# Expert weights of both layers as 1 MiB transfers throughout, where most went in pairs of 2 MiB

## The reference, cut to what matters

```python
def expert_choice_ffn(h, w_router, w_gate, w_up, w_down):
    b, n, d = h.shape
    cap = max(1, (EC_CAPACITY * n) // N_EXPERTS)          # 32 tokens for each expert
    aff = jax.nn.softmax((h @ w_router).astype(jnp.float32), axis=-1)
    g, idx = lax.top_k(jnp.swapaxes(aff, 1, 2), cap)
    xe = jax.vmap(lambda hb, ib: hb[ib])(h, idx)
    a = jnp.einsum('becd,edf->becf', xe, w_gate)
    up = jnp.einsum('becd,edf->becf', xe, w_up)
    y = jnp.einsum('becf,efd->becd', jax.nn.silu(a) * up, w_down) * g[..., None].astype(h.dtype)
    return jax.vmap(lambda ib, yb: jnp.zeros((n, d), h.dtype).at[ib.reshape(-1)].add(yb.reshape(-1, d)))(idx, y)
```

## Time and profile before

| | |
|---|---|
| median of 3 runs | 2635.04 us (2633.99 to 2636.32) |
| the profiled execution | 2635.41 us, its span 2634.1 us |
| PE busy | 2511.8 us (95%) |
| PEld (weight loads of PE) busy | 1543.5 us (59%) |
| DVE / ACT / POOL busy | 1182.1 / 437.4 / 92.7 us |
| moved by DMA | 690.06 MB, mean 262 GB/s |
| issued at line 745 in one piece of 2048 KB | 122 into `ring`, 9 + 9 + 8 into `ring_low`, `ring_high`, `ring_far` |
| granted clock of PE | 0.997 of full speed |

### The profile page before, as it was taken

One profiled execution on the slowest core, in us unless ns is written; L12 is line 12 of the kernel. 1 busy time (PEld: TensorE's weight loads), 2 busy tenths in 40 slices (PEclk: granted clock), 3 DMA queues, 4 the chain that ended last, 5 costly groups with the idle time before them and its releaser, 6 DMA issues.

```text
span 2634.1 us, 27251 instructions
## 1 busy us (share of the span) xinstructions
PE 2511.8 (95%) x11522; PEld 1543.5 (59%) x11522; DVE 1182.1 (45%) x1973; ACT 437.4 (17%) x878; POOL 92.7 (4%) x69
## 2 busy tenths in 40 slices
PE   9999999889999999987879999999999999999999
PEld 5344343424368843332338857888866875878884
DVE  4971321212165521110117755546656665553664
ACT  2111100001132210000001101531101111260110
POOL 0011000000000000000000110001001001001000
PEclk9999999999999999999999999999999999999999
DMA  9853999999962599999997653324444744333441
GB/s 370 323 221 156 393 427 425 428 427 428 425 279 79 205 365 428 427 426 428 426 424 230 194 191 144 112 86 191 171 176 156 196 176 160 128 112 128 170 181 65
DMA packets 93335, 690.06 MB, mean 262 GB/s; under 512 B 25621, under 2 KB 28053, under 8 KB 29469
## 3 DMA queue, kind: packets, MB, share of 16 engines
q1 hardware_dynamic: 90720, 682.66, 65.1%
q0 software_dynamic: 848, 2.90, 0.4%
q10 hardware_dynamic: 1644, 2.76, 0.3%
HBM read 687.22 MB, written 1.06 MB: 261 GB/s over the span
## 4 chain that ended last, share of the span: by engine, by line
PE 82%; DMA 12%; DVE 5%; issue 0%; ACT 0%; POOL 0%; DVEq 0%; POOLq 0%; ACTq 0%
PE bank L772 80%; DMA ring<-in_stream 9%; DMA ring_high<-in_stream 3%; PE bank L775 3%; DVE ab_z L2333 1%; DVE ring L2754 1%; DVE moe_turned L2522 0%; DVE moe_silu L2520 0%; DVE moe_results L2526 0%; DMA vectors<-in_vectors 0%; POOL ab_ln_sum L3058 0%; DVE moe_top L2437 0%; DVE gates L2715 0%; DVE moe_max L2435 0%; DVE normed L2706 0%
## 5 line engine op out<-in xcount | busy, mean ns | idle before, releaser
L772 PE MATMUL bank<-normed,ring 128*128 128x256 f32 (+1 forms) x1824 | 495.3, 428 | 5.0 <-ACT normed L1781 1.6
L772 PEld LDWEIGHTS bank<-normed,ring 128*128 128x128 f32 x1824 | 342.2, 190 | 152.0 <-issue 106.4
L772 PE MATMUL bank<-ring,gates 128*128 128x256 f32 (+1 forms) x1504 | 374.8, 393 | 2.1 <-DVE ring L2754 1.1
L772 PE MATMUL bank<-ring,moe_chosen 128*64 128x512 f32 x1504 | 334.3, 595 | 30.5 <-DMA ring<-in_stream 29.0
L772 PEld LDWEIGHTS bank<-ring,gates 128*128 128x128 f32 x1504 | 282.1, 190 | 60.8 <-issue 23.0
L772 PE MATMUL bank<-ring,normed 128*128 128x256 f32 (+1 forms) x1376 | 313.8, 375 | 0.5 <-DVE cd_rinv L2573 0.5
L772 PEld LDWEIGHTS bank<-ring,normed 128*128 128x128 f32 x1376 | 255.7, 190 | 36.7 <-issue 2.3
L772 PEld LDWEIGHTS bank<-ring,moe_chosen 128*64 128x64 f32 x1504 | 105.5, 137 | 247.9 <-issue 191.6
L2520 DVE TENSOR_TENSOR moe_silu<-bank,moe_silu 128x512 f32<-128x512 f32 x32 | 22.1, 691 | 408.1 <-PE bank L772 408.1
L772 PE MATMUL bank<-ring,moe_turned 128*64 128x512 f32 (+1 forms) x832 | 165.1, 547 | 19.8 <-DVE moe_turned L2522 18.0
L772 PE MATMUL bank<-ring,ffn_hidden 128*128 128x512 f32 x352 | 170.6, 592 | 0.0
(11 more groups left out here) (405 smaller groups left out, 2420.1 us busy)
## 6 DMA issues: line engine op xcount, KB each, us to landing
ring<-in_stream SPq DMA_DIRECT2D x296, 1024.0 KB, 6.9
ring<-in_stream SPq DMA_DIRECT2D x122, 2048.0 KB, 25.6
ring_low<-in_stream SPq DMA_DIRECT2D x9, 2048.0 KB, 39.9
ring_high<-in_stream SPq DMA_DIRECT2D x9, 2048.0 KB, 40.1
ring_far<-in_stream SPq DMA_DIRECT2D x8, 2048.0 KB, 38.2
hidden<-in_stream SPq DMA_DIRECT2D x10, 1024.0 KB, 36.0
normed<-in_stream SPq DMA_DIRECT2D x10, 1024.0 KB, 37.7
ring_filter_freq<-in_stream SPq DMA_DIRECT2D x6, 1024.0 KB, 16.6
```

The lines of the kernel that those rows point to most:

```text
L772: return nc.tensor.matmul(o, lhsT, rhs, start=start, stop=stop, skip_group_check=True)
```

## The change

`SINGLY` names all sixteen experts instead of two, for both layers, so that every entry of `transfers(plan)` is one chunk: each has its own wait, issue, landing semaphore and place in memory as 128 rows of 8 KB. `pack_stream`, which lays the stream out on the host, follows the same list. The order of the stream, the places, and all arithmetic stay as they are.

```diff
--- before.py
+++ after.py
@@ -353,7 +353,7 @@
 AB_COLUMN = {"gate_out": 0, "gate_in": 1, "val": 2, "glu_a": 3, "glu_g": 4}
 
 
-SINGLY = (1, 2)
+SINGLY = tuple(range(NE))
 
 
 def transfers(plan):
```

## The result

The changed kernel takes 2641.41 us (median of 9 runs, 2640.06 to 2642.74), the kernel before 2634.78 us in its 9 runs: ratio 1.0026, 95% interval 1.0018 to 1.0035. The forecast was 2641.9 us, slower than before. The profiled execution took 2641.10 us with a span of 2639.8, that is 5.7 us more than before in both.

A forecast was written before the change was run, and what follows sets the result against it. The prediction took the DMA engines, saturated in both expert stages, to bound the kernel. It added +10.6 us for the lower rate and -3.7 us for shorter tails to 2635.04 us, giving 2641.9 us, range 2635.0 to 2648.0.

The forecast's parts named there:

- The sum: Whole kernel: +10.6 us for the rate and -3.7 us for the tails, +6.9 us in all.
- What binds: Both expert stages: DMA engines never rest (busy share 1.01), so a stage ends when its bytes are through.
- Rival 3: Expert stages: PE's waits for landings set the end; removing 37.9 us of idle time gives 2597 us; chance 0.04.
- The rate: Saturated expert stages: each of 140 pairs costs 0.076 us more as two transfers, +10.6 us.
- The start: Start of both saturated stretches: unmoved, costed at nothing; at most 2.5 us at stake for each stage.
- Whose price it is: Saturated expert stages: shorter rows and a second completion together cost 0.076 us for each pair.
- The tails: Last up pair of each expert stage: half of PE's 3.68 us saved, -1.84 us each, -3.7 us in all.
- The issues: SP's queue: 148 added issues, 49 us, lie within its 2278.6 us of waiting for PE and cost nothing.
- Rival 1: Expert stages: half the price for each pair, +1.6 us in sum, 2636.6 us; chance 0.08.
- Rival 2: Expert stages: no price for the rate, only the tails count, 2.1 us saved, 2632.9 us; chance 0.08.
- Rival 4: Expert stages: single chunks run at 401 GB/s in bulk, +40 us, 2675 us; chance 0.07.
- Rival 5: Expert stages: a fixed 2.2 us for each transfer does not overlap, +308 us, 2943 us; chance 0.01.

The follow-up runs named there:

- experiment 3: The changed kernel, with PE waiting for both landings of a pair before its first matmuls on gate and up weights: 2645.3 us.
- experiment 1: The kernel before, its pairs kept as one transfer, wait and landing each, but moved as rows of 8 KB instead of 16 KB: 2645.4 us.
- experiment 2: The kernel before, each pair issued as two 1 MiB transfers after one wait, PE told only when both have landed: 2645.28 us.
- experiment 9: The kernel before with the change made for the first expert stage alone: 2637.72 us, ratio 1.0011 to the kernel before.
- experiment 4: The changed kernel with each expert chunk moved as 256 rows of 4 KB, still one 1 MiB transfer: 2667.44 us.

## Why the prediction was right, point by point

**The sum.** Forecast +6.9 us, measured +6.6 in the medians. That these agree within 0.3 us is partly luck: the profile has 5.7 us, made of 9.1 for the later landings and -3.4 for the tails, where the forecast had 10.6 and -3.7.

**What binds.** Right. The busy share stayed at 1.01, and every kernel with 8 KB rows ended its stages later by the bytes it moved at the lower rate. (One reading of the chain was off: of its ten DMA pieces nine lie in the expert stages, and one of 5.9 us at the very start of the program. Nothing hangs on it.) Rival 3, that PE's waits for landings set the end, fell: in the five groups of the earlier trace rows PE now idles 26.0 + 2.9 + 3.3 + 2.2 + 1.0 = 35.4 us for DMA instead of 37.9, and with the groups left out there 39.0 instead of 40.6, where the rival wanted nearly all of it gone; and experiment 3, which put the waits for pairs of gate and up weights back, cost the two tails and at most 0.5 us more.

**The rate.** Right in cause, a little large in size. The forecast's 0.076 us for a pair came from a 50 us window. Over 100 us, experiments 1 and 2 measure 0.072 and the changed kernel itself 0.073 (42.04 MB), 10.1 to 10.3 us for 140 pairs. The landings moved by a little less: in the changed kernel by 4.76 + 4.36 = 9.1 us, against 10.6 forecast, or 0.065 us a pair. Experiments 1, 2 and 3 have no gain at the tails and start the FFN 9.4, 10.1 and 9.7 us later than before (1392.51, 1393.23 and 1392.79 instead of 1383.13).

**The start.** Costed at nothing, and within 1 us it was. The first saturated stretch begins as before: no bytes in 267 to 269 us in both, 422 against 421 GB/s behind it. Ahead of the second the queue is idle in both, and bytes flow again some 2 us later than before, where the first stage ended 3.0 us later. Whether the separate waits gain something there is open. In the second stage alone, the two kernels with them lose 4.4 us (the changed kernel and experiment 3) and the two without 5.1 (experiments 1 and 2). But experiment 9, which has the pairs of before in that stage, also comes out 0.5 us better there than before, and one profile of each cannot settle it.

**Whose price it is.** The forecast named shorter rows and the second completion together. Experiments 1, 2 and 4 part them: rows of 16, 8 and 4 KB are moved at 427, 421 and 409 GB/s, whatever the number of transfers, and the completion costs nothing that the medians show. The single packets of the traces say the same. From 500 to 600 us a row of 16 KB takes 615.8 ns on its engine (before), one of 8 KB 314.1 (changed kernel), one of 4 KB 163.8 (experiment 4): two short rows take 12.4 and 13.5 ns longer than one of twice the length. A completion packet takes 9.6 ns. That the rates give only 9 ns a row goes with a busy share of 1.01 to 1.03: packets of one engine overlap a little. The Trainium skill, "DMA: Bandwidth & Descriptors", section "Why small descriptors are slow (HBM only)", has a fixed overhead for each packet; in kind the trace agrees, but the measured 1.5% of the transfer time is about twice the 0.8% that I estimated from that page, and it is plain at 8 and 16 KB.

**The tails.** Forecast -3.7 us, measured 2 x 1.7 = -3.4 by the 8 matmuls of 1.94 us where 16 of 3.65 were; half of 3.68 was slightly too much, since a part of the time, 0.2 us by these two figures, does not halve. Experiment 3 takes both away and pays 4.0. That the first stage's tail counts in full although PE had been idle only 0.29 us there was right too: with the landings 4.76 us later PE waits for each of the last three up chunks, 0.40 to 0.55 us.

**The issues.** Right: nothing. The issues into `ring_low` now take a median of 2.126 us, where it was 0.328; experiment 2, with as many transfers, has 2.124. The engines had work all the while (share 1.01), and only later weights stood behind SP.

**Rivals 1, 2, 4 and 5.** The price was 86% to 95% of the forecast, not half of it and not none. The rate of 401 GB/s did not become the rule (421 in bulk). A fixed cost that does not overlap would have been worth 308 us.

## What to carry to other kernels

Where the DMA engines never rest, a stage's length is its bytes through the rate, and the rate depends on the length of a row: compare windows with different transfers inside one trace before changing their size, multiply by what is issued inside the saturated stretch only, and add the work that stands behind the last landing. Cut transfers fine only where someone waits on them with nothing else to do: at the last landing of a stage, and perhaps behind an empty queue. Where one transfer alone is split, the gain is no more than the idle time in front of its landing. Make rows long everywhere else, but not so long that a transfer needs more free room than the slowest stretch of the consumer leaves, for then the queue runs empty, which costs more than the rows save.

## What I had not expected of the hardware

A row costs an estimated 9 ns on its engine even at 8 and 16 KB (12 to 14 ns by its packets), so that 427 GB/s was not yet the end: with part of the transfers in rows of 32 KB the rate was 428 and 429 GB/s. And a second completion for the same bytes, which I had counted into the price, shows in no median (2645.4 against 2645.28 us).
